# Seven block products for two more of 22 chunks, in an encoder's feed-forward blocks

## What is computed

```python
def swiglu(x, w_gate, w_up, w_down):
    return (jax.nn.silu(x @ w_gate) * (x @ w_up)) @ w_down      # 1024 -> 2816 -> 1024

def encoder_layer(x, ffn1, mix_pre_g, mixer_fn, mixer_params, mix_post_g, ffn2):
    pre1, wg1, wu1, wd1, post1 = ffn1
    x = x + FFN_RESIDUAL_WEIGHT * rms_norm(swiglu(rms_norm(x, pre1), wg1, wu1, wd1), post1)
    x = x + rms_norm(mixer_fn(rms_norm(x, mix_pre_g), *mixer_params), mix_post_g)
    ...
```

## Time and profile before

| | |
|---|---|
| Time, median of 3 runs | 2804.22 us (2801.74 to 2804.27) |
| The profiled execution's own time | 2805.26 us |
| Its span | 2803.2 us, clock 0.987 of full speed |
| Busy: PE, DVE, ACT, POOL | 96%, 51%, 35%, 57% |
| Chain that ended last, by engine | PE 80%, DVE 13%, issue 2%, ACT 2%, POOL 1% |

### The profile page before, as it was taken

The page is one execution under the profiler, slowest core; times in us unless marked ns, Lnnn a source line. Parts: engine busy times, 40 slices in busy tenths (PEclk is TensorE's granted clock), DMA queues, the critical chain, the costliest instruction groups (busy, mean ns, idle before and its releaser), DMA issues.

```text
span 2803.2 us, 36345 instructions
## 1 busy us (share of the span) xinstructions
PE 2687.4 (96%) x14266; PEld 2474.4 (88%) x14266; DVE 1431.5 (51%) x2564; ACT 983.8 (35%) x1644; POOL 1603.1 (57%) x870
## 2 busy tenths in 40 slices
PE   7999999989898999999999999998899999999998
PEld 7899999878678899999898999997799788999997
DVE  5643333659966643333664333337766476333335
ACT  4232332445443232332432322243344242323322
POOL 2576776559642576776536866683211244768665
PEclk9999999999999999999999999999999999999999
DMA  3222221311011222221421221240100211222213
GB/s 129 76 68 76 76 76 55 126 60 46 31 38 76 83 68 70 82 76 53 150 83 61 76 67 58 72 135 35 38 24 24 76 76 68 69 67 76 83 53 120
DMA packets 55320, 201.45 MB, mean 72 GB/s; under 512 B 6128, under 2 KB 6640, under 8 KB 55152
## 3 DMA queue, kind: packets, MB, share of 16 engines
q1 hardware_dynamic: 49104, 177.12, 19.0%
q10 hardware_dynamic: 6048, 22.02, 2.1%
HBM read 186.53 MB, written 12.58 MB: 71 GB/s over the span
## 4 chain that ended last, share of the span: by engine, by line
PE 80%; DVE 13%; issue 2%; ACT 2%; POOL 1%; ACTq 0%; DMA 0%; POOLq 0%; SPq 0%; DVEq 0%
PE ps L915 26%; PE ps L916 26%; PE ps L917 26%; DVE raw_sum L1543 2%; PE ps L1027 1%; DVE ps L1647 1%; DVE x L1561 1%; DVE sum L1543 1%; DVE y L1567 1%; DVE y L1550 1%; POOL w_lo L867 1%; DVE xn L1616 1%; POOL pacc L902 1%; PE ps L1012 1%; DVE pair L1593 1%
## 5 line engine op out<-in xcount | busy, mean ns | idle before, releaser
L867 POOL TENSOR_TENSOR w_lo<-w_stage,w_hi 128x1024 fp32r<-128x1024 f32 (+1 forms) x455 | 1014.8, 2258 | 636.4 <-ACT w_hi L1204 630.4
L915 PE MATMUL ps<-xn,w_hi 128*128 128x384 f32 x1920 | 649.5, 338 | 15.7 <-POOL w_lo L867 10.0
L916 PE MATMUL ps<-xn,w_hi 128*128 128x384 f32 x1920 | 645.9, 336 | 0.0
L917 PE MATMUL ps<-xn,w_lo 128*128 128x384 f32 x1920 | 645.2, 336 | 0.0
L1204 ACT ACTIVATE w_hi<-w_stage 128x1024 fp32r<-128x1024 f32 (+1 forms) x455 | 436.6, 983 | 80.1 <-POOL w_stage L878 55.4
L915 PE MATMUL ps<-w_hi,hid 128*128 128x512 f32 x1056 | 414.1, 392 | 12.4 <-issue 5.4
L917 PE MATMUL ps<-w_hi,hid 128*128 128x512 f32 x1056 | 411.4, 390 | 0.0
L916 PE MATMUL ps<-w_lo,hid 128*128 128x512 f32 x1056 | 411.2, 389 | 0.0
L915 PEld LDWEIGHTS ps<-xn,w_hi 128*128 128x128 f32 x1920 | 363.4, 189 | 20.2 <-POOL w_lo L867 10.8
L1550 DVE TENSOR_TENSOR y<-y,ps 128x512 f32<-128x512 f32 x264 | 180.2, 686 | 362.4 <-PE ps L917 362.4
L916 PEld LDWEIGHTS ps<-xn,w_hi 128*128 128x128 f32 x1920 | 363.3, 189 | 1.7
(11 more groups left out here) (188 smaller groups left out, 4051.9 us busy)
## 6 DMA issues: line engine op xcount, KB each, us to landing
w_stage<-weights SPq DMA_DIRECT2D x311, 512.0 KB, 3.6
x_kept<-x ACTq DMA_DIRECT2D x18, 512.0 KB, 2.6
x<-x_kept ACTq DMA_DIRECT2D x18, 512.0 KB, 7.0
g_pre<-rows SPq DMA_DIRECT2D x7, 512.0 KB, 5.6
x<-x_in SPq DMA_DIRECT2D x6, 512.0 KB, 8.6
g_post<-rows SPq DMA_DIRECT2D x6, 512.0 KB, 5.6
x<-x_in ACTq DMA_DIRECT2D x6, 512.0 KB, 8.0
y_out<-x SPq DMA_DIRECT2D x6, 512.0 KB, 2.6
```

The source lines that it names most:

```text
L867: pool.tensor_tensor(w_lo[:, s, 0:n], w_stage[:, s, 0:n], w_hi[:, s, 0:n].bitcast(F32), ALU.subtract).then_inc(w_split, 1)
L915: pe.matmul(out, a[0], m[0], start=start, stop=False)
L916: pe.matmul(out, a[0], m[1], start=False, stop=False)
L917: return pe.matmul(out, a[1], m[0], start=False, stop=stop)
```

## The change

Each FFN has two plain chunks instead of four, and 20 chunks instead of 18 go by seven products. Its first down block has two chunks instead of four, and the block of two in second place has four. So an FFN opens with four items instead of eight, and the sums of input blocks are laid out anew: steps 0 to 6 behind items 1 to 3, steps 7 to 12 between the twelve downs of the first block, and steps 13 to 15 behind the first three products of the first pair.

The opening is now the same for FFN and convolution: tile 3 is turned behind the first item, tile 4 in the middle of the second, and tile 5 behind the second. Tile 4 gets banks of its own (4 and 5), and the turns of tiles 3 and 5 wait for the turn two tiles before. The last tile's root stands behind the first item's product (`take` or `glu`) instead of in the middle of the first item. The groups of ring slots go on in turn from block to block, since an FFN now has an odd number of groups. SP's loads of the gain rows move from unit 9 of a block to unit 7, and the loads of units 6 and 7 of the first FFN wait for a free slot. The first turned latent waits for the turn of tile 5.

```diff
-FFN_BLOCKS = ((0, 4), (4, 2), (6, 4), (10, 4), (14, 4), (18, 4))
-PLAIN = 4
+FFN_BLOCKS = ((0, 2), (2, 4), (6, 4), (10, 4), (14, 4), (18, 4))
+PLAIN = 2
...
 def place_units():
+    free, turn = [list(range(4)), list(range(4, 8))], 1
     for b, kind in enumerate(SUBS):
         UNIT0.append(len(SLOT))
-        free, turn = [list(range(4)), list(range(4, 8))], 0
...
         if kind == "mla":
             SLOT.extend(MLA_SLOTS)
             LOADED.extend([True] * len(MLA_SLOTS))
+            assert turn % 2 == 0
+            free, turn = [list(range(4)), list(range(4, 8))], 0
...
-SUMS_BEHIND = {2: (0,), 3: (1, 2), 4: (3, 4, 5), 5: (6, 7, 8), 6: (9, 10, 11), 9: (12,), 12: (13,), 15: (14,), 18: (15,)}
+SUMS_BEHIND = {1: (0, 1, 2), 2: (3, 4, 5), 3: (6,), 4: (7,), 6: (8,), 8: (9,), 10: (10,), 12: (11,), 14: (12,)}
...
 def turn_bank(t):
-    return 2 if t == 2 else 6
+    return {2: 2, 4: 4}.get(t, 6)
...
             s.add(2.08, "pair", b, c, g, i, m)
+            if (c, g) == (PLAIN, 0) and i < 3:
+                s.add(0, "block_sum", b, 13 + i)
...
         for i, (c, half) in enumerate(order):
-            if i == 0:
-                middle = [("pre", b, 5)] if b > 0 else [("pre", 0, 3), ("enter", 4), ("pre", 0, 4), ("enter", 5), ("pre", 0, 5)]
-            else:
-                middle = []
-            if len(order) == 4 and i == 1:
-                middle = [("turn", b, 4)]
-            if len(order) == 8 and i == 3:
-                middle = [("turn", b, 5)] + [("spill", b, 5)] * (b > 0)
+            middle = []
+            if i == 0 and b == 0:
+                middle = [("pre", 0, 3), ("enter", 4), ("pre", 0, 4), ("enter", 5), ("pre", 0, 5)]
+            if i == 1:
+                middle = [("turn", b, 4)] + [("spill", b, 4)] * (SUBS[b] == "ffn" and b > 0)
             up(b, c, half, middle)
             s.add(0, "take" if SUBS[b] == "ffn" else "glu", b, c, half, s.q[b, c, half])
-            if len(order) == 4:
-                turn(b, (3, 5)[i]) if i < 2 else None
-            else:
-                if i in (1, 2):
-                    turn(b, i + 2)
+            if i == 0 and b > 0:
+                s.add(0, "pre", b, 5)
+            if i < 2:
+                turn(b, (3, 5)[i])
+            if SUBS[b] == "ffn":
                 for k in SUMS_BEHIND.get(i, ()):
                     s.add(0, "block_sum", b, k)
...
-                            for k in SUMS_BEHIND.get(8 + TILES * h + t, ()) if n == 0 else ():
+                            for k in SUMS_BEHIND.get(4 + TILES * h + t, ()) if n == 0 else ():
...
-            load(6)
-            load(7)
-            for u in [i for i in range(RING, UNITS) if LOADED[i]]:
+            for u in [i for i in range(6, UNITS) if LOADED[i]]:
...
-                    middle = UNIT0[b] + (KV_UNIT[1] if kind == "mla" else 9)
+                    middle = UNIT0[b] + (KV_UNIT[1] if kind == "mla" else 7)
...
-                    if t == 2 and b > 0:
-                        pe.wait_ge(y_done, work.out_end[b - 1] - 2)
-                    elif t != 2 and no > 0:
+                    if t in (2, 4) and b > 0:
+                        pe.wait_ge(y_done, work.out_end[b - 1] - (2 if t == 2 else 0))
+                    elif t in (0, 1) and no > 0:
                         pe.wait_ge(turn_done, 2 * (no - 1) + i + 1)
+                    elif t in (3, 5):
+                        pe.wait_ge(turn_done, 2 * (no - 2) + i + 1)
...
                 if t == 0:
-                    pe.wait_ge(y_done, work.out_end[3])
+                    pe.wait_ge(turn_done, 2 * norm_no(4, 5))
```

## The result

The changed kernel takes 2826.14 us (median of 4 runs, 2825.15 to 2827.73), the kernel before 2802.98 (4 runs): a ratio of 1.0083, 95% interval 1.0067 to 1.0099. The forecast was 2823.4. The profiled execution of the changed kernel took 2825.36, with a span of 2823.6 against 2803.2.

The account below looks back on a forecast made before the run. PE, busy 96% of the span, was taken to bound the kernel, with first down blocks deciding. FFNs +27.2, convolution -5.0, attention -3.0 make +19.2 on 2804.2: 2823.4 us, range 2798 to 2842.

Parts of the forecast that it names:

- Products: Each FFN: two plain chunks need 33.5 us, a pair by seven products 29.3; saves 4.2, four save 16.8.
- Opening: Four items, two turns, 3.7 us gap ahead of item 2, 1.2 clock loss: 40.0 us an FFN, the first 42.2.
- the rule: A VectorE block-sum step stands until GpSimd's running instruction ends, then runs whole (1.75 us), while GpSimd's next one stands.
- First down block: Twelve downs of two chunks with steps 6 to 12 between them take 26.5 us, bounds 20.9 and 32.6; the deciding term.
- the waits for GpSimd in these seven steps sum to 5.6: First down block, steps 6 to 12: VectorE waits 5.6 us for GpSimd; without them the count ends at 20.9.
- the count on record: The prediction's step-by-step timing of a first down block from the last item's end: step 6 ends at 6.0, twelfth down 26.5.
- VectorE keeps pace: Rival, first down blocks: GpSimd's instructions fall under PSUM copies, 30.4 us less, 2793; below 2800, chance 0.14.
- half clock in the downs: Rival, first down blocks: PE's stops halve its clock, 32.6 us instead of 26.5, 24 more, 2848; above 2836, chance 0.10.
- Behind it: After the first down block: the second group's product 1 waits 2.0 us for GpSimd's third w_lo; bound below 0.
- Convolution: Turn 4's stop of 3.28 us for turn 3's low parts and the slow running behind it go: 5.0 us saved.
- At nothing: Costed at zero: SP's row loads two units forward, first FFN's loads 6 and 7, the ring across blocks, latent turn's wait.
- Attention: Turn 4 stood 5.28 us for the same reason as the convolution's; between 0 and 5.3 saved, 3.0 taken.

Follow-up runs that it names:

- experiment 3: Changed kernel with block-sum steps 6 to 11 cut to additions of 8 columns in the three later first down blocks: 2810.78 us, 1.0025 of before.
- experiment 4: Changed kernel with GpSimd's eight instructions in the three later first down blocks cut to 8 columns each: 2820.24 us, 1.0058 of before.
- experiment 5: Changed kernel with eight of a first down block's twelve evictions on ACT, steps 6 to 12 behind VectorE's four: 2833.22 us, 1.0107 of before.
- experiment 1: Changed kernel with the convolution's gain rows loaded ahead of unit 9 again instead of unit 7: 2823.35 us, 1.0067 of before.
- experiment 2: Kernel before with only the new opening, turn banks and waits; four plain chunks, old blocks, sums, ring, loads and rows: 2780.47 us, 0.9918 of before.

## Why the prediction came out right, and where it didn't

The forecast (slower, 2823.4) stood 2.7 us from the time, and its main step held: the first down block decides, because VectorE has steps and evictions there (experiment 3 took steps out, and the block fell to 18.4 us). But the closeness of the sum is luck. Against +20.4 between the spans the forecast had +19.2, and its terms missed by more than that: the FFNs by -5.2, the convolution by +7.1, attention by +2.1, the start by -2.5.

**Products.** 168 and 192 matmuls, as counted.

**Opening.** Forecast 42.2 and 40.0; measured 42.46, 40.52, 43.87, 40.51. The gap behind turn 5 was put at 3.7: it is 3.71 in the third FFN (886.94 to 890.65). Clock loss was put at 1.2; 13 matmuls in the next 3.85 us where 22 fit are 1.6:

```profile
890.65:894.50 3.85, 3.85 (x13) 3.85 (x14) 3.78 (x3) 0.00 (x0) 0.00 (x0) 0.56 0.00 0
```

The fourth FFN missed by 3.9, by a wait I hadn't seen: VectorE's root chain of the tile before. Its instructions on 128 x 2 elements take 0.16, but these two stand beside `w_lo`:

```profile
1405.47 2.31 DVE L1597 TENSOR_TENSOR pair<-pair 128x2 f32<-128x2 f32 x1
...
1408.40 2.29 DVE L1605 TENSOR_TENSOR pair<-pair 128x2 f32<-128x2 f32 x1
```

```profile
1405.38 2.38 POOL L866 TENSOR_TENSOR w_lo<-w_stage,w_hi 128x1024 fp32r<-128x1024 f32 x1
1408.27 2.40 POOL L866 TENSOR_TENSOR w_lo<-w_stage,w_hi 128x1024 fp32r<-128x1024 f32 x1 [0.52 <-ACT w_hi L1206]
```

Each ends when GpSimd's instruction does (1407.78 and 1407.76; 1410.69 and 1410.67). My prediction had the rule from the earlier trace rows and applied it to the block sums alone. No run took this wait away, so it is read, not tried.

**First down block.** Forecast 26.5, measured 23.75 to 25.65. The count without GpSimd (20.9) is 1 to 3 us below what experiment 4 measured (21.86, 23.70 and 22.08), where the clock still fell. The term that was mis-sized is "the waits for GpSimd in these seven steps sum to 5.6": in the third FFN the seven steps take 15.1 us for 12.25, so 2.9, and experiment 4 gives 2.5 a block. VectorE, GpSimd and PE in that block:

```profile
911.80 1.98 DVE L1545 TENSOR_TENSOR sum<-raw_sum,sum 128x1536 fp32r<-128x1536 f32 x1
914.30 2.22 DVE L1545 TENSOR_TENSOR raw_sum<-sum,xn 128x1536 f32<-128x1536 f32 x1
917.67 1.75 DVE L1545 TENSOR_TENSOR raw_sum<-sum,xn 128x1536 f32<-128x1536 f32 x1
...
921.36 1.94 DVE L1545 TENSOR_TENSOR raw_sum<-raw_sum 128x1536 f32<-128x1536 f32 x1
924.41 2.75 DVE L1545 TENSOR_TENSOR sum<-raw_sum,sum 128x1536 fp32r<-128x1536 f32 x1
927.08 1.27 DVE L1557 COPY y<-ps 128x512 f32<-128x512 f32 x2
```

```profile
910.87 1.30 POOL L876 TENSOR_TENSOR w_stage<-w_stage 128x512 f32<-128x512 f32 x1
912.10 2.80 POOL L877 TENSOR_TENSOR w_stage<-w_stage 128x512 f32<-128x512 f32 x1
914.86 2.79 POOL L879 TENSOR_TENSOR w_stage<-w_stage 128x512 f32<-128x512 f32 x1
917.79 14.35 POOL L866 TENSOR_TENSOR w_lo<-w_stage,w_hi 128x1024 fp32r<-128x1024 f32 x4
```

```profile
914.43 0.50 PE L914 MATMUL ps<-w_hi,hid 128*128 128x512 f32 x1 [2.57 <-DVE y L1557]
```

Step by step, 6 to 12, the waits are 0.2, 0.5, 0, 0.2, 1.0, 1.0 and 0; the count on record has 1.25, 0.7, 1.2, 1.2, 1.2, 0.1 and 0. So the rule held, and what was wrong is when the two meet. GpSimd began 0.55 us after the last item (909.49), not 0.25, and step 6 met the end of its second sum instead of nearly the whole third. Step 8 then came just as the fourth sum ended (917.65), where the count had a `w_lo`. Step 9 came late, because VectorE had itself waited 0.67 for PE. Only steps 10 and 11 paid about the 1.2 of the count: two copies cover half of a `w_lo`, and the step waits for the other half. GpSimd pays more than VectorE: three `w_lo` of 2.4 and a half one of 1.3 take 14.35 us for 8.5. The rival "VectorE keeps pace" came half true, and experiment 5 shows what happens when the copies are gone.

In return the rival "half clock in the downs" came half true. Behind the first stop the clock fell, and PE's busy time in the block is 19.2 us for 17.0 in experiment 3:

```profile
914.00:916.00 2.00, 1.57 (x5) 1.24 (x6) 2.00 (x2) 1.06 (x2) 2.00 (x2) 0.71 0.00 0
916.00:918.00 2.00, 1.76 (x5) 0.97 (x4) 2.00 (x4) 1.26 (x2) 1.86 (x2) 0.50 0.00 0
...
920.00:925.00 5.00, 4.48 (x21) 3.38 (x20) 4.33 (x6) 1.49 (x1) 5.00 (x2) 1.00 0.00 0
```

It didn't swing: once it was back at 1.00, later stops of 0.5 to 0.85 us in this block left it there, and in the fourth FFN's block one of 2.07 (ahead of 1455.59). So the Trainium skill's case (TensorE: Matmul & The Clock Gate, section A second HAM failure mode: psum-queue depth-cycling), short idles between groups of matmuls that make the clock swing, isn't what this block shows.

**Behind it.** The 2.0 us wait for the second group's third `w_lo` came in the fourth and the last FFN, at 0.82:

```profile
1485.31 0.44 PE L914 MATMUL ps<-sum,w_hi 128*128 128x384 f32 x1 [0.82 <-POOL w_lo L866]
```

The first and the third have a stop of 0.78 for `u_sum` instead. The two pairs take 59.8 to 59.9 where 60.6 was forecast: 0.8 less an FFN. With 1.8 less for the mean down block (24.7) that is 10.3 for four; the openings take 5.2 more than forecast, most of it the fourth FFN's; so +22.0 in place of +27.2.

**Convolution.** Forecast -5.0; measured +0.6 from item 0 to item 2 (27.85 for 27.26), and a longer slow stretch behind it, +2.1 in all. The step that failed stands under "At nothing": the row loads were costed for the FFNs, where they are indeed covered, and not for the convolution, whose unit 7 SP issues while the last root is still under way. Put back (experiment 1), the load no longer stops it, and item 0 to item 2 takes 24.20, 3.1 less than before: PE still stands 0.77 ahead of turn 4 and 0.85 ahead of turn 5. In experiment 2 these two stops are gone as well, and the saving is 5.1.

**Attention.** Forecast -3.0; measured -0.9 over the whole stretch. Turn 4's stop fell from 5.28 to 1.13, but turn 5 stands 2.34, and turn 0 now stands 3.02, where it had no stop, again behind a root chain beside `w_lo`:

```profile
1911.73 2.32 DVE L1597 TENSOR_TENSOR pair<-pair 128x2 f32<-128x2 f32 x1
1914.09 2.30 DVE L1599 TENSOR_TENSOR pair<-pair 128x2 f32<-128x2 f32 x1
```

```profile
1918.74 1.54 PE L1013 MATMUL ps<-ident,y 128*128 128x128 f32 x6 [3.02 <-DVE y L1569]
```

From where turn 0 was due to the product behind turn 5 it is 47.5 us for 46.3. That stop ahead of turn 0 is in all ten kernels with 20 chunks and in neither of the two with 18 and the new opening. It may be the ring that runs on across blocks, costed at nothing: it moves GpSimd's `w_lo` in time against VectorE's roots. No run changed the ring alone, so this isn't shown.

**Start.** The first item starts 2.5 us earlier, as it does in the other kernels with the new opening, also in the one that keeps loads 6 and 7 up front (20.36 in experiment 2). VectorE's scaling of tile 2 shows most of it, first in the kernel before, beside GpSimd's `w_lo`, then in the changed kernel:

```profile
15.88 3.35 DVE L1567 SCALAR_TENSOR_TENSOR y<-x,stat,g_pre 128x1024 f32<-128x1024 f32 x1
```

```profile
13.47 4.67 POOL L867 TENSOR_TENSOR w_lo<-w_stage,w_hi 128x1024 fp32r<-128x1024 f32 x2 [13.02 <-ACT w_hi L1204]
```

```profile
15.19 1.49 DVE L1569 SCALAR_TENSOR_TENSOR y<-x,stat,g_pre 128x1024 f32<-128x1024 f32 x1
```

Before, the scaling came as GpSimd's second `w_lo` began and stood for all of it; after, it came 0.7 us earlier and met only the end of the first. That is 1.9 of the 2.5, read from one trace of the kernel before. The other 0.7 is input tiles that landed earlier (ACT's second square starts at 8.12 for 8.82), and why they did stays open.

## What to carry to other kernels

When work moves into a stage, cost it against every engine that holds something there for its whole length, and look for all instructions of that kind, the smallest too: a 128 x 2 addition that had to stand took 2.3 us, more than a block-sum step alone (1.75). Before moving work off a busy engine, ask what its other instructions were separating: taking eight copies away from VectorE let its steps collide fully with GpSimd, while taking the last four, with fewer steps left, paid. And measure a change's parts apart: here the reordered opening alone was worth 24 us, and the rest of the change hid it. Where an account ends close to the time, compare it term by term: here terms that missed by 2 to 7 us added up to 1.2.

## What the runs showed of the hardware

- VectorE's additions with both inputs in SBUF stood until GpSimd's running instruction ended, at every size seen (128 x 2, 128 x 8, 128 x 1536): 2.3 us for 128 x 2 elements that take 0.16 alone, beside a `w_lo` of 2.4; in experiment 3 an addition of 128 x 8 elements took 2.08 (at 916.91). The rule is the Trainium skill's (SBUF — State Buffer, section Who interferes with whom: a VectorE instruction with two SBUF inputs contends with a GpSimd instruction that reads SBUF, and the blocked one stands fully); the size of the loss depends on what lies between: 2.9 us in seven steps with copies out of PSUM between them, 7.8 in six steps without.
- PE's clock fell behind a stop of 2.57 us among the third FFN's downs and one of 2.68 ahead of its item 2, and not behind later stops of 0.5 to 0.85 in that down block, nor behind the 2.07 in the fourth FFN's. The last FFN before stopped 2.27 us and stayed at 1.00; experiment 4's third FFN stopped 2.34 us ahead of its third down (913.64), and the next 2.36 us read 0.53.
